# Two neighbouring S5 states side by side in memory: runs or strides of 8 bytes in place of 512

## What is computed

```python
bu_re = jnp.einsum('btgp,gnp->btgn', u, bb_re)      # inputs of the recurrence, per group
bu_im = jnp.einsum('btgp,gnp->btgn', u, bb_im)
# s[t] = a * s[t-1] + bu[t], complex, elementwise, over t = 0..255
_, _, s_re, s_im = lax.associative_scan(combine, (a_re, a_im, bu_re, bu_im), axis=1)
y = (jnp.einsum('btgn,gpn->btgp', s_re, c_re)
     - jnp.einsum('btgn,gpn->btgp', s_im, c_im) + d_skip * u)
```

## Time and profile before

| | us |
|---|---|
| median of 3 runs | 2986.1 (2983.25 to 2987.63) |
| the profiled execution, its own time | 2986.08 |
| its span in the profile | 2984.3 |
| S5 stretch: first step of the scan to the end of the last `outputs` | 1117.4 to 1534.7 |
| of it, PE busy before the last two `outputs` | all but 6.8 and 3.7 |

### The profile page before, as it was taken

How to read it: one execution, slowest core, us unless ns; L and a number is a source line. 1 busy time by engine, 2 the same in 40 slices (tenths; PEclk the granted TensorE clock), 3 DMA queues, 4 the chain that set the end, 5 groups by cost and what they waited for, 6 DMA issues and landing times.

```text
span 2984.3 us, 47457 instructions
## 1 busy us (share of the span) xinstructions
PE 2900.1 (97%) x19639; PEld 2086.5 (70%) x19639; DVE 912.0 (31%) x2066; ACT 517.6 (17%) x809; POOL 100.5 (3%) x179
## 2 busy tenths in 40 slices
PE   8999999999999999999999999999999999999996
PEld 7888788888888888888888888873444444444442
DVE  1433424424334307777730000130121112111214
ACT  2221222222212132111010000121111111112110
POOL 2010011000100000000000000000000000000000
PEclk9999999999999999999999999999999999999998
DMA  6243342332434524244347665258899999999996
GB/s 195 81 131 99 98 125 91 101 123 80 138 94 113 154 95 136 92 127 128 122 145 218 197 194 171 112 204 361 362 422 422 422 422 422 422 422 422 422 422 261
DMA packets 325775, 654.05 MB, mean 219 GB/s; under 512 B 45232, under 2 KB 274736, under 8 KB 275440
## 3 DMA queue, kind: packets, MB, share of 16 engines
q1 hardware_dynamic: 325616, 651.61, 59.4%
HBM read 649.49 MB, written 2.10 MB: 218 GB/s over the span
## 4 chain that ended last, share of the span: by engine, by line
PE 58%; issue 16%; DVE 12%; DMA 6%; DVEq 2%; ACT 1%; POOLq 1%; POOL 1%; SPq 1%; ACTq 0%
PE bank L938 11%; PE bank L632 10%; PE bank L1108 9%; PE bank L1142 7%; DMA arena<-in_w_up_dram 6%; DVE arena L1759 4%; PE bank L1086 4%; PE bank L972 4%; PE bank L1165 4%; DVE arena L1761 3%; DVE arena L1763 3%; PE bank L706 1%; PE bank L724 1%; PE bank L717 1%; PE bank L1119 1%
## 5 line engine op out<-in xcount | busy, mean ns | idle before, releaser
L632 PE MATMUL bank<-arena 128*128 128x256 f32 x4096 | 934.0, 383 | 0.0
L632 PEld LDWEIGHTS bank<-arena 128*128 128x128 f32 x4096 | 765.3, 190 | 112.6 <-issue 8.0
L1108 PE MATMUL bank<-arena 128*64 128x512 f32 x2048 | 447.0, 595 | 6.2 <-DMA arena<-in_w_up_dram 6.2
L1108 PEld LDWEIGHTS bank<-arena 128*64 128x64 f32 x2048 | 145.1, 137 | 306.1 <-issue 290.1
L938 PE MATMUL bank<-arena 128*128 128x256 f32 x1536 | 331.8, 379 | 0.0
L938 PEld LDWEIGHTS bank<-arena 128*128 128x128 f32 x1536 | 291.8, 190 | 39.9 <-issue 0.3
L1142 PE MATMUL bank<-arena 128*64 128x512 f32 x1024 | 223.3, 594 | 7.7 <-ACT masks L1466 7.7
L877 PE MATMUL bank<-arena 128*128 128x256 f32 x1024 | 223.5, 380 | 0.0
L877 PEld LDWEIGHTS bank<-arena 128*128 128x128 f32 x1024 | 194.0, 190 | 27.3 <-issue 1.0
L1142 PEld LDWEIGHTS bank<-arena 128*64 128x64 f32 x1024 | 72.1, 137 | 148.5 <-issue 137.0
L2023 DVE TENSOR_SCALAR arena<-bank 128x512 f32<-128x512 f32 x16 | 11.1, 692 | 473.7 <-PE bank L1108 473.7
(11 more groups left out here) (307 smaller groups left out, 2001.4 us busy)
## 6 DMA issues: line engine op xcount, KB each, us to landing
arena<-in_w_in_dram SPq DMA_DIRECT2D x72, 2048.0 KB, 8.7
arena<-in_w_up_dram SPq DMA_DIRECT2D x64, 2048.0 KB, 15.9
arena<-in_w_gate_dram SPq DMA_DIRECT2D x64, 2048.0 KB, 13.4
arena<-in_w_down_dram SPq DMA_DIRECT2D x64, 2048.0 KB, 20.6
arena<-in_w_dn_out_dram SPq DMA_DIRECT2D x16, 2048.0 KB, 8.5
arena<-in_w_glu_b_dram SPq DMA_DIRECT2D x8, 2048.0 KB, 8.2
arena<-in_w_glu_a_dram SPq DMA_DIRECT2D x8, 2048.0 KB, 8.3
arena<-in_w_mix_out_dram SPq DMA_DIRECT2D x8, 2048.0 KB, 13.7
```

What stands on the lines that cost most here:

```text
L632: last = mm(ps[bank][:, ct * T:ct * T + T], ring[:, buf, k, ct * P:ct * P + P], rhs[:, k, :], start=k == 0, stop=k == KD - 1)
L1108: last = mm(ps[bank][CAP * o:CAP * o + CAP, :], xg[:, 4 * q + k, CAP * o:CAP * o + CAP], w[:, o, k], start=False, stop=q == 3 and k == 3, ...
```

## The change

SS becomes (32 pairs, 2 parts, 64 columns, 2 steps of the pair). Two neighbouring steps of a column lie side by side (8 bytes), pairs lie 1024 bytes apart, and columns of one step lie 8 bytes apart where they were 4 apart. The state before a chunk moves out of SS into a place of its own, S_before, in the old layout.

- `outputs`: the moving operand is 32 runs of 2 numbers in place of 64 single numbers. Count and shapes of the products stay.
- `fill` and `help_fill`: the copies write runs of 2 numbers in place of single ones.
- `scan`: L1759 reads the state before, and the two additions read and write their state, at a stride of 8 bytes in place of 4. The products, `prod` and `rot`, stay packed. The first 8 steps of each chunk are written out ahead of the loop, since the first one reads S_before.
- the copy of the last state between chunks reads with a stride of 8 bytes.

```diff
-        SS = (at(SS0, STEPS + 1, 2, NJ), at(2 * KD * SC, STEPS + 1, 2, NJ))
+        SS = (at(SS0, STEPS // 2, 2, NJ, 2), at(2 * KD * SC, STEPS // 2, 2, NJ, 2))
+        S_before = at(SS0 + STEPS * 2 * NJ, 2, NJ)
...
-                            last = mm(ps[2][32 * i:32 * i + 32, k * STEPS:k * STEPS + STEPS],
-                                      CT[:, c, 8 * kh + k, 32 * i:32 * i + 32], SS[ch % 2][:, 1:STEPS + 1, c, j],
+                            last = mm(ps[2][32 * i:32 * i + 32, k * STEPS:k * STEPS + STEPS]
+                                      .rearrange("p (r e) -> p r e", e=2),
+                                      CT[:, c, 8 * kh + k, 32 * i:32 * i + 32], SS[ch % 2][:, :, c, j],
                                       start=c == 0, stop=c == 1)
...
-                view = SS[ch % 2][:, 1:STEPS + 1].rearrange("p t c (k i) -> p c i k t", i=4)
+                view = SS[ch % 2].rearrange("p r c (k i) e -> p c i k r e", i=4)
...
-                    nc.scalar.copy(view[:, c, i, 8 * kh:8 * kh + 8], ps[4 + i][:, :].rearrange("p (k t) -> p k t", k=8))
+                    nc.scalar.copy(view[:, c, i, 8 * kh:8 * kh + 8],
+                                   ps[4 + i][:, :].rearrange("p (k r e) -> p k r e", k=8, e=2))
...
+            def step(prev, cur):
+                V.tensor_tensor(prod, prev.unsqueeze(2).to_broadcast([P, 2, 2, NJ]), rot, ALU.mult)
+                dve.drain()
+                V.tensor_tensor(cur, cur, prod[:, 0], ALU.add)
+                dve.drain()
+                V.tensor_tensor(cur, cur, prod[:, 1], ALU.add)
+                dve.drain()
+
             def scan(ch, lo, hi):
-                with dve.Fori(lo // 8, hi // 8) as t8:
-                    some = SS[ch % 2][:, ds(8 * t8, 9)]
+                states = SS[ch % 2]
+                if lo == 0:
+                    step(S_before, states[:, 0, :, :, 0])
+                    for t in range(1, 8):
+                        step(states[:, (t - 1) // 2, :, :, (t - 1) % 2], states[:, t // 2, :, :, t % 2])
+                with dve.Fori(max(lo // 8, 1), hi // 8) as t8:
+                    some = states[:, ds(4 * t8 - 1, 5)]
                     for t in range(8):
-                        prev, cur = some[:, t], some[:, t + 1]
-                        V.tensor_tensor(prod, prev.unsqueeze(2).to_broadcast([P, 2, 2, NJ]), rot, ALU.mult)
...
+                        step(some[:, (t + 1) // 2, :, :, (t + 1) % 2], some[:, (t + 2) // 2, :, :, t % 2])
...
-                    V.tensor_copy(SS[(ch + 1) % 2][:, 0], SS[ch % 2][:, STEPS])
+                    V.tensor_copy(S_before, SS[ch % 2][:, STEPS // 2 - 1, :, :, 1])
```

More of the change, by code:

```diff
@@ L1749, in _ @@
             dve.wait_ge(s5_trc, 16)
-            V.memset(SS[0][:, 0], 0.0)
+            V.memset(S_before, 0.0)
             dve.drain()
             dve.sem_inc(merged_ready, 1)
-            def scan(ch, lo, hi):
-                with dve.Fori(lo // 8, hi // 8) as t8:
-                    some = SS[ch % 2][:, ds(8 * t8, 9)]
-                    for t in range(8):
-                        prev, cur = some[:, t], some[:, t + 1]
-                        V.tensor_tensor(prod, prev.unsqueeze(2).to_broadcast([P, 2, 2, NJ]), rot, ALU.mult)
[L1760 to L1764, removed]
+            def step(prev, cur):
[5 more added lines that the diff above has]
+                dve.drain()
+            def scan(ch, lo, hi):
+                states = SS[ch % 2]
[5 more added lines that the diff above has]
+                    some = states[:, ds(4 * t8 - 1, 5)]
+                    for t in range(8):
+                        step(some[:, (t + 1) // 2, :, :, (t + 1) % 2], some[:, (t + 2) // 2, :, :, t % 2])
             def finish(ch):
@@ L1786, in help_fill @@
             def help_fill(c):
-                view = SS[0][:, 1:STEPS + 1].rearrange("p t c (k i) -> p c i k t", i=4)
+                view = SS[0].rearrange("p r c (k i) e -> p c i k r e", i=4)
                 dve.wait_ge(bu_ready, 3 + c)
                 for i in (2, 3):
-                    V.tensor_copy(view[:, c, i, 8:16], ps[4 + i][:, :].rearrange("p (k t) -> p k t", k=8))
+                    V.tensor_copy(view[:, c, i, 8:16], ps[4 + i][:, :].rearrange("p (k r e) -> p k r e", k=8, e=2))
                 dve.drain()
```

## The result

| | before | after |
|---|---|---|
| median of 4 runs each, us | 2984.68 (2981.47 to 2987.63) | 2944.89 (2942.47 to 2950.35) |
| the profiled execution | 2986.08 | 2944.4 |
| its span | 2984.3 | 2942.7 |

The ratio is 0.9871, 95% interval 0.9855 to 0.9887. The gain is 39.8 us by the medians and 41.6 us by the two spans; 31.4 were forecast.

A forecast was written before the change was run, and what follows sets the result against it. PE, held up with DVE by its strided reads, was taken as the bound; 2.7 (first wait) + 25.0 (outputs) + 3.7 (last wait) = 31.4 us off 2986.1 gave 2954.7, range 2938 to 2976 (0.85).

The forecast's parts named there:

- What bounds the kernel: S5 stretch: PE busy 97% of the span, DVE's scan nearly as long beside it; PE's strided reads hold up both.
- The waits: PE's waits for the scan before outputs: the first falls from 6.8 to 4.1 us, the last, 3.7 us, goes.
- The size of a call: Outputs on PE: a call falls from 7.0 to 3.9 us, bounds 1.8 and 7.0; eight calls save 25.0 us.
- the pace of L841: Outputs estimate from the inputs products, also 64 columns wide and four side by side: 128 x 31.4 ns, 4.0 us per call.
- The lower bound, 1.8 us: Outputs call as if the array were the limit, from L632's time: 14 ns per product four side by side.
- One fetch per jump: Outputs call if each address jump costs one fetch: halving the jumps halves the time, to 3.5 us.
- DVE's stalls: Scan instructions held up during six outputs calls, 30 us too much; 10 us taken as left, bounds all or none.
- The scan's stride: DVE's scan at 8 bytes instead of 4: no cost taken; upper bounds 336 ns per step for reads, 256 for writes.
- Behind the stretch: L938, the router and the experts after the S5 stretch move forward by as much as the stretch gains.
- A: Rival: DVE's stalls stay whole, tied to the number of fetches of the states; gain 13.4 us, 2972.7; chance 0.08.
- B: Rival: pairs don't help; outputs stay at 7.0 us and stalls at 30; gain 6.4 us, 2979.7; chance 0.07.
- C: Rival: the scan's wider stride costs DVE, kernel slower from 169 ns per step, 3028.8 at the reads' bound; chance 0.09.

## Why the prediction was right, and where it was off

**What bounds the kernel**: right. PE's strided reads held up PE and DVE both, and changing them alone removed both effects.

**The waits**: right. For the first one 4.1 us was forecast and 4.21 measured; its parts too, the last two copies at 1.11 us against 1.17, and the scan to its end 1.2 us shorter against 1.5. The last wait went, as said. DVE took 277 us from the start of the first outputs to the end of the last scan, where 278 had been worked out for no stalls at all.

**The size of a call**: this step failed. The term was 3.9 us, and 2.65 was measured, so the saving is 34.8 us instead of 25.0. I had taken the pace of L841 because it has the same width and fourfold packing. But its four products lie side by side by rows (32*128 in the trace: 32 rows, 128 columns each), those of outputs by columns (128*32), so it is another form, and it isn't a bound for this one: the new calls take 2.5 us for 128 records, 19.5 ns each, where L841 takes 31.4. The lower bound, 1.8 us, was sound and nearer; whole runs come to 1.99. "One fetch per jump", half of 7 us, was wrong as well, since 3 of the 7 us are not the jumps but the collision, which no row of before showed apart.

**DVE's stalls**: the term was 10 us left, 0.8 were measured. The direction was right, the size not. It had no consequence: at either value DVE is done ahead of PE, 1493 against 1494.8 by the forecast, 1479 against 1484.3 in the trace.

**The scan's stride**: right at zero. Of the bounds, the reads' own, 0.66 ns more per number, was too low: at 16 bytes it is 0.75. What was wrong was to think of a cost that grows with the distance. It jumps between 8 and 16 bytes, and then hardly grows. The zero was taken for nearness to 4, and it held because 8 bytes lies on the free side of the jump: the value was right, that reason for it was luck.

**The gap in the last call**: not foreseen, 2.6 us lost. It came back in both later traces of the changed kernel and in those of three variants with calls as short (2.42 to 3.35 us), with 0.51 us in the one whose last call has singles 64 bytes apart, and in none whose last call is longer than 5 us. In the trace a packet of the instruction queue runs in this call; in the kernel before such a packet met a call of 7 us. That PE used up its instructions faster than the next ones came is a likely cause. Runs of four, with a last call of 1.99 us, have no gap: there PE had stood idle for 27 us just before, time enough for a fetch. The DMA load is a rival, alone or together with this: its share in the last call was 0.84 to 0.92 in the traces with a gap of 2.4 us and more, 0.68 in the one with 0.51, and at most 0.25 in all without a gap, runs of four with 0.00 among them. Short calls and a loaded DMA came together in every trace, and no run moved the fetch or the load, so the cause of the gap stays open.

**Behind the stretch**: right; everything moved forward by as much.

The sum of the forecast was 31.4: with 9.8 more for the calls, 2.6 less for the gap, and 3.0 of scatter ahead of the stretch it comes to the 41.6 of the two spans. The gap, which no term held, hid a quarter of what the calls' term was short of.

**Rivals.** A fell with PE's read changed alone. B fell: pairs bring 7.0 to 2.65. C is real at 16 bytes, with its place and price, and did not occur at 8.

The Trainium skill, page "SBUF — State Buffer", section "Door 1: The DMA port swizzle", says that lines are 16 bytes and that two accesses to the same line are enough for full bandwidth. The runs agree in the main: two numbers per 16 bytes cost DVE nothing and PE 2.20 us against 1.99, one costs 618 ns against 426 and 3.99 us against 1.99. They differ where the section lets fp32 stride over four numbers for free: a distance of four numbers, 16 bytes, pays the whole cost.

The same page, section "SBUF: two separate sides", says that only DVE and GpSimd wait for each other and that PE and DVE never do. The measurement decides against it here: with GpSimd idle, a DVE addition of 0.29 us lasted 7.51 us under PE's read, and 30 us of such stalls vanished when nothing but PE's addresses was changed.

## What to carry to other kernels

If an instruction is longer than its median only while another engine reads with a stride, change that engine's addresses before anything else: two numbers side by side, a distance that isn't a power of two (one was tried, 516 bytes), or side-by-side products that read 32 bytes and more apart. Then look at which chain of similar length runs beside it, because a layout that is still better for one engine can cost the other more: runs of four took 0.6 us more off a call of PE and lost 50 us by DVE. Price a new operand form by a single experiment with one form per call, not by the row that looks most alike.

## What the runs showed of the hardware

- PE, four 64-column fp32 products side by side, 128 records: 1.99 us for runs of 16 bytes and more, 2.20 for singles at 8 bytes, 4.0 for singles at 16 to 64 bytes and at 516.
- At 128, 256, 512 and 1024 bytes the same call takes 5.8, 6.6, 6.5 to 7.6 and 6.6 us with the four products 4 bytes apart. At 512 bytes it is 5.5 to 6.3 if the real and the imaginary parts lie 128 bytes apart in place of 256, 8.0 if the four products read the same numbers, 3.77 if they are 32 bytes apart.
- With pairs every 1024 bytes it is 2.56 us with the four products 8 bytes apart and 2.03 with 64.
- PE's reads can hold up DVE, up to 7.51 us for one instruction. In the changed kernel the longest scan instruction is 497 ns.
- DVE reads fp32 at 8 bytes as fast as at 4, and at 16 to 256 bytes at a surcharge of 0.65 to 0.77 ns per number, 1.02 for the additions at 256.
- ACT's copy of 128x512 out of a bank takes 1097 ns where it writes 512 bytes apart, 624 with pairs, 599 with runs of four, 585 packed.
